# Reordering the last expert of a mixture-of-experts kernel and changing how its result is summed

## The reference

```python
hid = silu(t @ expert_w_gate[g, e]) * (t @ expert_w_up[g, e])    # 256 wide, only the tokens routed to (g, e)
y  += combine[:, g, e] * (hid @ expert_w_down[g, e])              # two experts a token
h   = layer_norm(DEEPNORM_ALPHA * h + y, ln2_g, ln2_b)            # the kernel's output
```

## Time and profile before

| | us |
|---|---|
| median of 3 runs | 834.0 (833.46, 834.0, 834.1) |
| profiled execution, its own time | 834.92 |
| its span, first to last instruction | 833.2 |
| PE busy | 772.1 (93%) |
| DVE, ACT, POOL busy | 487.4, 377.1, 49.6 |
| mean granted TensorE clock | 0.968 |

### The profile page before, as it was taken

The page is one execution under the profiler, slowest core; times in us unless marked ns, Lnnn a source line. Parts: engine busy times, 40 slices in busy tenths (PEclk is TensorE's granted clock), DMA queues, the critical chain, the costliest instruction groups (busy, mean ns, idle before and its releaser), DMA issues.

```text
span 833.2 us, 16271 instructions
## 1 busy us (share of the span) xinstructions
PE 772.1 (93%) x6690; PEld 642.0 (77%) x6690; DVE 487.4 (58%) x843; ACT 377.1 (45%) x573; POOL 49.6 (6%) x91
## 2 busy tenths in 40 slices
PE   6999999999999999999999999999999876877776
PEld 6999998999999998999998999899855332333332
DVE  4455567767676678867764444486875423323335
ACT  4556664545544556467553554464432211111123
POOL 0200032000000000100110000000010000000000
PEclk9999999999999999999999999999999989778889
DMA  8964453555556654534343132459989999999993
GB/s 281 303 211 129 150 161 105 187 169 199 181 175 199 192 170 144 191 113 153 118 137 102 53 105 100 152 174 403 408 342 409 407 409 409 409 409 409 409 408 148
DMA packets 102482, 194.36 MB, mean 233 GB/s; under 512 B 4669, under 2 KB 70560, under 8 KB 102288
## 3 DMA queue, kind: packets, MB, share of 16 engines
q1 hardware_dynamic: 99952, 186.66, 62.1%
q0 software_dynamic: 1888, 4.61, 1.7%
q10 hardware_dynamic: 576, 2.14, 0.7%
HBM read 192.35 MB, written 1.05 MB: 232 GB/s over the span
## 4 chain that ended last, share of the span: by engine, by line
PE 72%; DMA 15%; DVE 5%; SPq 4%; ACT 2%; issue 1%; ACTq 0%; DVEq 0%
PE PG L2047 15%; PE PG L2049 14%; PE PG L2048 14%; DMA expert_w<-in_expert_w_up 10%; DMA expert_w<-in_expert_w_down 4%; SPq L678 4%; PE PG L2651 3%; PE PM L2047 3%; PE PM L2049 3%; PE PM L2048 3%; PE PM L2503 1%; PE PG L2674 1%; ACT whi L850 1%; PE PM L2682 1%; PE PG L2114 1%
## 5 line engine op out<-in xcount | busy, mean ns | idle before, releaser
L2047 PE MATMUL PG<-hT_hi,whi 128*128 128x256 f32 (+1 forms) x816 | 235.5, 289 | 0.2 <-DVE hT_lo L1380 0.2
L2049 PE MATMUL PG<-hT_hi,wlo 128*128 128x256 f32 (+1 forms) x816 | 230.5, 282 | 0.0
L2048 PE MATMUL PG<-hT_lo,whi 128*128 128x256 f32 (+1 forms) x816 | 230.4, 282 | 0.0
L1363 DVE TENSOR_TENSOR wlo<-raw,whi 128x2048 fp32r<-128x2048 f32 x73 | 167.2, 2291 | 66.5 <-ACT whi L850 66.4
L2047 PEld LDWEIGHTS PG<-hT_hi,whi 128*128 128x128 f32 x816 | 153.9, 189 | 6.5 <-issue 3.1
L2049 PEld LDWEIGHTS PG<-hT_hi,wlo 128*128 128x128 f32 x816 | 154.1, 189 | 0.0
L2048 PEld LDWEIGHTS PG<-hT_lo,whi 128*128 128x128 f32 x816 | 153.5, 188 | 0.2
L850 ACT ACTIVATE whi<-raw 128x2048 fp32r<-128x2048 f32 x73 | 139.4, 1910 | 22.0 <-PE PG L2049 19.7
L2651 PE MATMUL PG<-expert_w,xw 128*32 128x256 f32 x992 | 74.3, 431 | 25.1 <-DMA expert_w<-in_expert_w_up 24.9
L2651 PEld LDWEIGHTS PG<-expert_w,xw 128*32 128x32 f32 x992 | 30.5, 119 | 55.2 <-DMA expert_w<-in_expert_w_up 28.9
L1958 DVE SCALAR_TENSOR_TENSOR y_lo<-PG,small,y_hi 128x512 fp32r<-128x512 f32 x16 | 12.0, 750 | 73.8 <-ACT y_hi L1282 73.8
(11 more groups left out here) (525 smaller groups left out, 1345.2 us busy)
## 6 DMA issues: line engine op xcount, KB each, us to landing
expert_w<-in_expert_w_gate SPq DMA_DIRECT2D x64, 512.0 KB, 15.4
expert_w<-in_expert_w_up SPq DMA_DIRECT2D x64, 512.0 KB, 15.7
expert_w<-in_expert_w_down SPq DMA_DIRECT2D x32, 1024.0 KB, 17.1
raw<-in_ffn_w_up SPq DMA_DIRECT2D x22, 1024.0 KB, 5.1
raw<-in_w_in SPq DMA_DIRECT2D x22, 1024.0 KB, 5.0
raw<-in_moba_w_qkv SPq DMA_DIRECT2D x12, 1024.0 KB, 6.0
raw<-in_ffn_w_down SPq DMA_DIRECT2D x11, 1024.0 KB, 4.9
raw<-in_moba_w_o SPq DMA_DIRECT2D x4, 1024.0 KB, 5.1
```

Source lines behind the costliest of these rows:

```text
L1363: dve.tensor_tensor(lo_of(n), raw[:, n % R, :], hi_of(n).bitcast(F32), ALU.subtract).then_inc(s_lo, 1)
L2047: pe.matmul(dst, lh, rh, start=start, stop=False, **kw)
L2048: pe.matmul(dst, lh, rl, start=False, stop=False, **kw)
L2049: return pe.matmul(dst, ll, rh, start=False, stop=stop, **kw)
```

## The change

Four edits, all in the handling of expert 31:

- SP issues (30,2) before (31,0), no longer after (31,1). The queue's end becomes (30,0) (30,1) (29,2) (30,2) (31,0) (31,1) (31,2) lnrow2, with the same number of DMAs.
- PE runs `add_of(29)` and `down(30)` before `gate_up(31)`. Between the two halves of `gate_up(31)` it runs `add_of(30)` and `add_tokens` for all four banks. `transposes(31)` and `down(31)` follow the second half directly.
- ACT's `tokens_hi` moves behind `result_out` of expert 30, and DVE's `tokens_lo` behind `result_lo` of expert 30; DVE's `slots_of(31)` follows `tokens_lo`, and `product(31)` comes after it.
- Expert 31's result isn't split into hi and lo. Down is done in two groups of 256 columns, one in bank PG[0], one in PG[3]; ACT scales the first and DVE the second, each into float32 `last_y`; and `add_last` sums with four float32 matmuls in place of eight F32R ones.

```diff
@@ SP
             for e in range(NU, NE):
+                if e == NE - 1:
+                    sp.wait_ge(s_duse, e - NU)
+                    expert_load(e - 1, 2, (e - 1) % NU)
                 for kind in range(2):
                     sp.wait_ge(s_guse, 2 * (e - NU) + kind + 1)
                     expert_load(e, kind, e % NU)
-                if e > NU:
+                if NU < e < NE - 1:
                     sp.wait_ge(s_duse, e - NU)
                     expert_load(e - 1, 2, (e - 1) % NU)
@@ ACT
                     if e == NE - 1:
+                        of_last_but(e)
                         tokens_hi(NE - 1)
                     act.wait_ge(s_guse, 2 * e + 2)
                     sums_out(e % 2)
...
-                act.wait_ge(s_duse, NE)
-                act.activation(last_y[:, 0, :], last_result, ACT.Copy, scale=slotw[(NE - 1) % 2]).then_inc(s_yhi, 1)
+                act.wait_ge(s_dn, 1)
+                act.activation(last_y[:, 0:D // 4], last_result[0], ACT.Copy, scale=slotw[(NE - 1) % 2]).then_inc(s_yhi, 1)
@@ DVE
+                for e in range(NE - 1):
...
-                    if e == NE - 2:
-                        tokens_lo()
-                dve.wait_ge(s_slotw, NE)
-                dve.wait_ge(s_yhi, NE)
-                dve.scalar_tensor_tensor(last_y[:, 1, :], last_result, slotw[(NE - 1) % 2], last_y[:, 0, :].bitcast(F32),
-                                         ALU.mult, ALU.subtract).then_inc(s_y, 1)
+                e = NE - 1
+                of_last_but(e)
+                tokens_lo()
+                dve.wait_ge(s_duse, e)
+                slots_of(e, 0, e % 2, e, hot[e % 3])
+                dve.wait_ge(s_sg, e + 1)
+                product(e % 2)
+                dve.wait_ge(s_duse, NE)
+                dve.tensor_scalar(last_y[:, D // 4:D // 2], last_result[1], slotw[e % 2], None, ALU.mult).then_inc(s_y, 1)
@@ PE, in gate_up
                     if last_window:
                         mm.then_inc(s_guse, 1)
+                    if between is not None and kind == 0:
+                        between()
@@ PE
+            def add_last(hot):
+                for t in range(TT):
+                    for h in range(2):
+                        x = slice(BLK * h, BLK * h + BLK)
+                        mm = pe.matmul(PM[:, 2 * t + h, :], hot[x, P * t:P * t + P].bitcast(F32), last_y[x], start=False, stop=True)
+                    mm.then_inc(s_sum, 1)
...
-                for e in range(NE):
+                for e in range(NE - 1):
...
-                add_tokens((0, 1))
-                pe.wait_ge(in_ring[(NE - 1) % NU][2], 16 * ((NE - 1) // NU + 1))
+                e = NE - 1
+                add_of(e - 2)
+                down(e - 1)
+                pe.wait_ge(s_win, e)
+                pe.wait_ge(s_back, e - 1)
+
+                def between():
+                    add_of(e - 1)
+                    add_tokens((0, 1, 2, 3))
+
+                gate_up(e % NU, xw[e % 2], e % 2, e // NU + 1, True, between=between)
+                pe.wait_ge(s_gu, NE)
+                transposes(e % 2)
+                pe.wait_ge(in_ring[e % NU][2], 16 * (e // NU + 1))
                 pe.wait_ge(s_hm, NE)
-                down_of((NE - 1) % NU, (NE - 1) % 2, s_duse, last_result)
-                add_of(NE - 2)
-                add_tokens((2, 3))
+                w = ring[e % NU][2][:, :].rearrange("p (f n) -> p f n", f=2)
+                for b, done in enumerate((s_dn, s_duse)):
+                    for f in range(2):
+                        for h in range(2):
+                            q = WIN * (2 * h + f)
+                            c = D // 2 * h + D // 4 * b
+                            mm = pe.matmul(last_result[b][q:q + WIN, :], hid2[e % 2][:, f, :], w[:, f, c:c + D // 4], start=True, stop=True)
+                    mm.then_inc(done, 1)
                 pe.wait_ge(s_back, NE)
+                pe.wait_ge(s_yhi, NE)
                 pe.wait_ge(s_y, NE)
-                add(hot[(NE - 1) % 3], False, True, ys=[last_y[:, n, :] for n in range(2)])
+                add_last(hot[e % 3])
                 last_rows_out()
```

More of the change, by code:

```diff
@@ L537, in build @@
         res_lo = place("res_lo", [P, TT, D], 21248, F32R)
-        last_y = place("last_y", [P, 2, D // 2], 79616 + 4096, F32R)
+        last_y = place("last_y", [P, D // 2], 79616 + 4096)
         spare_sq = place("spare_sq", [P, 2, D // 2], 79616 + 8192)
@@ L609, in build @@
         gate_upT, result = PG[:, 2, 0:SEQ].rearrange("p (j n) -> p j n", j=2), PG[:, 3, :]
-        last_result = PG[:, 0, :]
+        last_result = [PG[:, b, 0:D // 4] for b in (0, 3)]
         QKV_ORDER = [(0, 0), (1, 0), (2, 0), (0, 1), (1, 1), (2, 1), (0, 2), (1, 2), (0, 3), (1, 3), (2, 2), (2, 3)]
@@ L1297, in narrow, with of_last_but @@
             def narrow():
+                def of_last_but(e):
+                    act.wait_ge(s_slotw, e)
+                    act.wait_ge(s_duse, e)
+                    result_out((e - 1) % 2, y_of(e - 1)[0], result.rearrange("p (q n) -> p q n", n=P))
                 for e in range(NE):
                     if e == NE - 1:
+                        of_last_but(e)
                         tokens_hi(NE - 1)
@@ L1304, in narrow @@
                         rows_out()
[L1305 to L1308, removed]
+                    if 0 < e < NE - 1:
+                        of_last_but(e)
                     act.wait_ge(s_T, e + 1)
@@ L1960, in narrow, with of_last_but @@
             def narrow():
-                for e in range(NE):
-                    if e == NE - 1:
-                        dve.wait_ge(s_sg, e + 1)
-                        product(e % 2)
-                    if e > 0:
[L1966 to L1971, removed]
+                def of_last_but(e):
+                    dve.wait_ge(s_slotw, e)
+                    dve.wait_ge(s_yhi, e)
+                    result_lo((e - 1) % 2, y_of(e - 1), result.rearrange("p (q n) -> p q n", n=P))
+                for e in range(NE - 1):
+                    if e > 0:
+                        of_last_but(e)
+                    dve.wait_ge(s_sg, e + 1)
+                    product(e % 2)
                     if e == 0:
@@ L2638, in rest_of_slots, with gate_up @@
                         features_of_slots(k, t)
-            def gate_up(u, x, i2, landings, last_window, slots_in=False):
+            def gate_up(u, x, i2, landings, last_window, slots_in=False, between=None):
                 for kind in range(2):
@@ L2730, in narrow @@
                         add_of(e - 3)
-                    if e > 1 and (e % 2 == 0 or e == NE - 1):
+                    if e > 1 and e % 2 == 0:
                         add_of(e - 2)
```

## The result

| | kernel before | changed kernel |
|---|---|---|
| median | 834.06 (833.46 to 835.18, 8 runs) | 836.26 (835.65 to 837.8, 8 runs) |
| ratio | | 1.0021, 95% interval [1.0012, 1.0030] |
| profiled execution, span | 834.92, 833.2 | 836.53, 834.7 |

What follows compares the result with a forecast made beforehand. Loads bound the kernel until the last landings, then PE, ACT and DVE. +3.29 for the later `down(31)`, -1.60 for the unsplit result, +0.29 for the float32 sum: +1.98, so 836.0; own range 835.4 to 836.6, wider 834.8 to 838.0.

Steps and rivals of the forecast that it cites:

- What bounds: Whole kernel: loads at 409 GB/s set the pace until the last landings, then PE, ACT and DVE set the end.
- two waits for loads: Old tail: PE waited for (31,1) until 812.07 and for (31,2) until 817.19; the new order removes both.
- The new wait: Between the halves of `gate_up(31)`: PE waits for expert 30's result, done 814.21; second half starts 817.50, 2.9 late.
- The hop: Each engine-to-engine step on the new path takes 0.12 us; 0.05 off would count five times, 0.25.
- Given back at the end, 1.60: From `down(31)` to the last sum: the unsplit result takes 1.73 in place of 3.33, giving back 1.60.
- The float32 pair: Last sum: float32 matmuls on two row halves overlap, so tile 0's `bn_stats` starts 1.16 after it, not 0.87; +0.29.
- Tile 1: Second tile of the last sum: ready 0.86 after tile 0, 2.02 after the sum's start, at 824.23; +2.45.
- ACT's path: After the last sum: ACT's root has 0.45 slack against DVE, which the later second tile uses up; cost 0.0.
- The hidden work: Rival: work between the halves of `gate_up(31)` hides behind the load; end moves -0.9, 833.1, no change; chance 0.07.
- the series: Rival: the float32 sum's row halves run one after the other; +3.7 in all, 837.7; chance 0.08.
- The clock: Rival: PE falls to its lower level in the exposed work from 810 to 822 us; +2.5, 838.5; chance 0.12.
- the range's top of 838.0: Upper end of the forecast's wider range, 834.8 to 838.0, which left out the top of the lower-clock case.

Runs made afterwards that it cites:

- the second profile: Changed kernel without further edit, profiled again beside the follow-up runs and tabulated step by step against the forecast; `bn_stats` of tile 0 at 823.32, forecast 823.37.
- the one with slack: Against the changed kernel: residual made during expert 30, three banks added before `add_of(29)`, one behind `down(31)`, nothing between the halves; 834.02, 0.9988 of the kernel before.

## Why the prediction was right

- **What bounds.** The loads do until the tail and PE, ACT and DVE behind them, as said; that PE's new order needs the new order of the last loads is shown by the old load order (+6.8); the new loads with PE's old order were not run. One reading of the old path was off, at no cost to the sum: the forecast has two waits for loads on it and takes 817.19 for a landing. The idle time there is 0.36, as long as at 819.31 where no load is awaited, and the old chain has one such wait, at 814.58, and no DMA piece behind it.
- **The new wait.** `between` waits for expert 30's lo part, the chain through expert 29's and 30's results is the one forecast, and the last half starts at 817.37 (forecast 817.50) with no load as releaser. Without the residual there it starts 2.0 sooner in the trace.
- **The hop.** The price of 0.12 for every engine-to-engine step fits three kinds of step and is too much for two. In the second profile it is 0.12 from the product to down's weight load and from `last_y` to the sum's, 0.13 from ACT's hi part to DVE's lo part, but 0.05 from the lo part to `add_of` and 0.06 from ACT's sums to the transposes. The two steps to `add_of` are why the table runs 0.13 ahead of the forecast from its first row on.
- **Given back at the end, 1.60.** The sum of the step holds (1.76 from down to the sum, forecast 1.73), its attribution doesn't: 1.04 is the unsplit result, the rest the earlier `slotw`. The forecast had read the 3.33 of before as three steps in series and missed that wait. In the old order the same edit gives nothing.
- **The float32 pair.** +0.39 (1.26 from the weight load to `bn_stats` in both profiles, in place of 0.87), forecast +0.29; the halves do overlap. Tile 1 starts 2.05 after the sum (forecast 2.02), and ACT's path costs nothing.
- **The rivals.** The hidden work and the series are excluded by the timelines. The clock didn't fall behind 804 us in either profile of the changed kernel. It did in others of the new order (0.63 from 804 to 808 in the one with slack) and of the old (0.50 there in three), and single runs of the changed kernel up to 840.17 lie above the range's top of 838.0. That these are clock falls wasn't seen in their own traces. The forecast named this for 810 to 822 us only; the exposed stretch begins at 804.

## What to carry to other kernels

When a queue of loads sets the pace, work on the compute engines before the last landings is free as far as their idle time there reaches, and a reordering that removes the wait for one load can put all of that work on the end's path; work out where the new path last touches a load, and what stands between it and the end. A faster form of the last step gains nothing while its consumer is still busy, so take the consumer's other work (here the residual) out of the tail first. Some slack before the last landing can absorb a low clock: one trace shows it, the medians don't decide it.

## What the runs showed of the hardware

- With the split result in the new order, PE's clock fell to its lower level (0.50) in the tail after waits of its own: 1.76 us of PE work in the 4 us from 820 to 824, then 3.78 us for float32 matmuls that take 1.98 at full level.
- A low clock behind a load costs nothing while PE has idle time before the next one: with 0.50 from 804 to 808 expert 30's down still started at 814.63 in the old order. With 1 us of PE work more, and 0.72 from 808 to 812, it didn't (815.44).
- Float32 matmuls on two row halves overlap: from the weight load of a pair of 512 columns to its reader it is 1.26, of one full-array matmul 1.16. From the first matmul's start it is 1.23 for the pair, and 0.60 for a single-pass pair.
- The whole stream of loads shifts between executions: the last half of expert 30's gate and up starts at 804.40, 803.70, 804.39 and 805.90 in the four profiles of the kernel before, the changed one (twice) and the best one. That is as much as most effects studied here, so such traces are compared from a landing and not from the span's start.
